# Latent attention: the rotation of the queries moved into the score's sum, and the copies of turned weights moved to one engine

## The chip, the cores and the metric

The kernel runs on one core of a Trainium2 chip. The metric is the device time of one execution in microseconds (us). A core has a matrix engine (TensorE, PE in the profile), a vector engine (VectorE, DVE), an activation engine (ScalarE, ACT), a general engine (GpSimd, POOL) and an engine that here issues the loads (SyncE, SP). Each works through its own instructions in order and waits on semaphores for the others.

## The reference, cut to what matters

One inference step of a backbone with two layers on 640 tokens (512 latent ones and 128 of a prompt). Each layer makes an adaptive norm, three attentions side by side (differential, latent, windowed), a gated merge of their outputs, and a mixture of 16 experts. The change touches the latent attention alone, which has 8 heads:

```
cq = (rms_norm(m_q, q_norm) @ mla_w_qb).reshape(B, S, 8, 64 + 32)
q_nope, q_rope = cq[..., :64], cq[..., 64:]
if latent: q_rope = apply_rope(q_rope); kr = apply_rope(kr)      # pairs (x1, x2) -> (x1 c - x2 s, x1 s + x2 c)
kv = (ckv @ mla_w_kvb).reshape(B, Sk, 8, 64 + 64)                # 64 key columns, 64 value columns a head
k = concat(kv[..., :64], kr for every head)
o = softmax(q k^T * 96 ** -0.5) v
```

Latent queries see 512 latent keys and 128 of a context (640 in all); the queries of the prompt see their own 128 keys.

## The kernel before, in words

All is fp32. In the latent attention queries and keys lie turned: features in partitions, tokens along the free dimension. A head is five steps, one for each tile of 128 queries (t = 0 to 4; t = 4 is the prompt's tile with 128 keys, the others have 640). A step i has a **score** (`mla_score`, L1029, called S below: PE writes 128x640 into `mm`), a **move** (`mla_move`, L2089: VectorE brings it into SBUF and takes the maximum), an **exponential** (`mla_exp`, L1594, on ScalarE), a **turn** (`mla_turn`, L1037, called T: five PE transposes into the one PSUM tile `tp`), a **copy** (`mla_copy`, out of `tp` into `ml_pt`, on ScalarE for even i, at L1356, and on VectorE for odd i, L2097), and, for one or two tiles together, the **values** (`mla_value`, L1049, called V, and a transpose of the inverse sums, L1053). The code writes out the order of each engine by hand: in the loop over s, PE makes the score of step s, then the turn of step s - 2, then the values of the unit that step s - 3 completes (so V falls at t = 1, 2 and 4).

Between the scores PE also prepares the next head. `project_head` has three pieces: piece 0, the queries (`product` at L749, 96 rows out, called P0), at t = 1; piece 1, the 64 key rows (L1000, P1), at t = 2; piece 2, a multiplication of the 32 query rows by a constant that swaps each pair (L1005, P2), at t = 3. ScalarE brings P0 and P1 into SBUF (`head_in`) ahead of the exponential of t = 1 and t = 2. VectorE makes the rotation of the 32 rows in `rope_head`: ahead of the move of t = 3 the swapped rows times the sine, behind that move the rows times the cosine and the sum (all at L1814). The copy of an odd step stands behind that on VectorE.

Scores and pieces share two PSUM tiles `mm`, taken in turn: the n-th user waits till the user before the last has been read (`wait_mm_empty`). A turn waits till the copy before it has emptied `tp` and till its exponential is done.

Ahead of the heads stand the rotation of the shared key rows (L974 on PE, `rope` on VectorE, and a copy to the second key buffer at L2071), and the values of all heads (`mla_v`, L987). Weights come through a ring of six slots: SP loads a chunk when the GpSimd program, by `consumed`, has counted its slot free. GpSimd computes nothing in the loops; it only counts. Chunk `qb` holds the query weights (256 rows in two halves, 768 columns), `kvb` the others.

Of the kernel before, what the change touches and what calls it, by code (L numbers as in the profile page):

```python
# [22 lines left out]
P = 128  # L23
# [5 lines left out]
TT = T // P  # L29
# [31 lines left out]
def _layout(parts):  # L61
# [9 lines left out]
    ("iota", CAP_L), ("cos64", NLAT), ("sin64", NLAT), ("cos32", NLAT), ("sin32", NLAT)])  # L71
# [7 lines left out]
def shape_constants():  # L79

    t = np.zeros((P, CONST_COLS), np.float32)

    def put(name, rows, value):
        a, b = CONST[name]
        t[rows, a:b] = value

    p = np.arange(P)
    put("ident", slice(0, P), np.eye(P))
    swap = np.zeros((P, P), np.float32)
    swap[p[1::2], p[0::2]] = -1.0  # L90
# [24 lines left out]
    put("cos32", slice(MNOPE, MQ), np.cos(a32))  # L115
    put("sin32", slice(MNOPE, MQ), np.sin(a32))
    lam = np.array([[0.8 - 0.6 * math.exp(-0.3 * l) for l in range(DEPTH)]]).T
    lam = np.concatenate([lam, 1.0 - lam], axis=1).astype(np.float32)
    return t, lam
# [47 lines left out]
def _turns(parts):  # L167
# [14 lines left out]
    ("mla_heads", MLA_N + 3 * MH), ("mla_out", 16), ("sw_kv_rot", 7),  # L182
# [88 lines left out]
def mla_s(i):  # L271


    h, t = divmod(i, TT)
    return MM["mla_heads"] + 3 + h * (TT + 3) + t + (min(t, 3) if h < MH - 1 else 0)


def mla_prep(h, piece):

    return MM["mla_heads"] + (piece if h == 0 else 3 + (h - 1) * (TT + 3) + 1 + 2 * piece)  # L280
# [48 lines left out]
def build(nc, a):  # L329
    ctx = ExitStack()  # L330
    with ctx:
# [174 lines left out]
        c_normed, kr_ready, mq_roped = sem("c_normed"), sem("kr_ready"), sem("mq_roped")  # L506
# [86 lines left out]
        def _(sp):  # L593
# [5 lines left out]
            def chunk_source(l, kind, k0, c0, width):  # L599
                r0 = k0 * P  # L600
                if kind == "qb":
                    return a["mla_w_qb"][l].rearrange("(k p) c -> p k c", p=P)
                if kind == "kvb":
                    return a["mla_w_kvb"][l]
                w = {"ada": "w_ada", "in": "w_in", "gate": "w_gate", "br_da": "w_br_da",
                     "br_mla": "w_br_mla", "br_swa": "w_br_swa", "o": "w_o"}[kind]
                return a[w][l, r0:r0 + HALF * P, c0:c0 + width].rearrange("(k p) c -> p k c", p=P)

            def chunk_target(kind, slot, width):
                if kind == "qb":  # L610
                    return ring[slot][:, :, :].rearrange("p k c -> p (k c)")[:, 0:2 * MH * MQ].rearrange(
                        "p (k c) -> p k c", k=2)
                if kind == "kvb":
                    return ring[slot][:, :, :].rearrange("p k c -> p (k c)")[:, 0:MH * (MNOPE + MV)]
                return ring[slot][:, :, 0:width]

            for l in range(DEPTH):
# [15 lines left out]
                def load(i):  # L633
                    kind, k0, c0, width = CHUNKS[i]

                    sp.wait_ge(chunks_free, l * LAYER_CHUNKS + (i + 1))
                    if i == FIRST["in"] + 2:

                        sp.dma_start(a["x_spill"], x[:, :, :]).then_inc(x_spilled, 16)
                    sp.dma_start(chunk_target(kind, i % RING, width),  # L640
                                 chunk_source(l, kind, k0, c0, width)).then_inc(slot_in[i % RING], 16)
# [50 lines left out]
        def _(pool):  # L692
# [6 lines left out]
            for l in range(DEPTH):  # L699
# [14 lines left out]
                consumed(SW_Q[3], 2)  # L714
                consumed(mla_prep(MH - 1, 2), 2)
# [17 lines left out]
        def _(pe):  # L733
# [103 lines left out]
            for l in range(DEPTH):  # L837
# [126 lines left out]
                for m in range(4):  # L964
# [15 lines left out]
                wqb = ring[FIRST["qb"] % RING][:, :, :].rearrange("p k c -> p (k c)")[:, 0:2 * MH * MQ].rearrange(  # L980
                    "p (k c) -> p k c", k=2)
# [8 lines left out]
                def project_head(hd, piece):  # L990
                    j = mla_prep(hd, piece)
                    if piece == 2:
                        wait_mm_read(pe, l, mla_prep(hd, 0))
                    wait_mm_empty(pe, l, j)
                    if piece == 0:
                        product(mm[j % 2][0:MQ, :], lambda k: wqb[:, k, hd * MQ:(hd + 1) * MQ],
                                lambda k: cq[:, k, :], 2).then_inc(mm_full[j % 2], 1)
                    elif piece == 1:
# [4 lines left out]
                    else:  # L1003
                        pe.sem_inc(pe_waited, 1)
                        pe.matmul(mm[j % 2][MNOPE:MQ, 0:NLAT], c_("swap32", slice(MNOPE, MQ)),  # L1005
                                  ml_q[hd % 2][MNOPE:MQ, 0:NLAT], start=True, stop=True).then_inc(mm_full[j % 2], 1)
# [7 lines left out]
                for piece in range(3):  # L1014
                    project_head(0, piece)
# [3 lines left out]
                def mla_score(i):  # L1019
                    hd, t = divmod(i, TT)  # L1020
                    if 1 <= t <= 3 and hd < MH - 1:
                        project_head(hd + 1, t - 1)
                    if t == 0:
                        wait_mm_read(pe, l, mla_prep(hd, 1))
                        pe.wait_ge(mq_roped, l * MH + (hd + 1))
                    j = mla_s(i)
                    wait_mm_empty(pe, l, j)
                    for lo, hi, at in latent_keys(t):
                        last = pe.matmul(mm[j % 2][:, at:at + hi - lo], ml_q[hd % 2][0:MQ, t * P:(t + 1) * P],  # L1029
                                         ml_k[hd % 2][0:MQ, lo:hi], start=True, stop=True)  # L1030
# [323 lines left out]
        def _(act):  # L1354
# [60 lines left out]
            for l in range(DEPTH):  # L1415
# [164 lines left out]
                def head_in(hd, piece):  # L1580
                    j = mla_prep(hd, piece)
                    wait_mm_full(act, l, j)
                    if piece == 0:
                        copy(ml_q[hd % 2][0:MQ, :], mm[j % 2][0:MQ, 0:T], -(MQ ** -0.5)).then_inc(mm_empty[j % 2], 1)
                    else:
                        copy(ml_k[hd % 2][0:MNOPE, :], mm[j % 2][0:MNOPE, 0:KEYS]).then_inc(mm_empty[j % 2], 1)

                head_in(0, 0)
                head_in(0, 1)
# [14 lines left out]
                for s in range(MLA_N + 2):  # L1604
                    if s < MLA_N:
                        hd, t = divmod(s, TT)
                        if 1 <= t <= 2 and hd < MH - 1:
                            head_in(hd + 1, t - 1)
                        mla_exp(s)
                    if s >= 2 and s % 2 == 0:  # L1610
                        mla_copy(s - 2)
# [200 lines left out]
        def _(dve):  # L1812
# [92 lines left out]
            for l in range(DEPTH):  # L1905
# [165 lines left out]
                dve.tensor_copy(ml_k[1][r32, :], ml_k[0][r32, :]).then_inc(kr_ready, 1)  # L2071

                def rope_head(hd, part):

                    j = mla_prep(hd, 2)
                    t_, q_ = tmp[j % 2][r32, 0:NLAT], ml_q[hd % 2][r32, 0:NLAT]
                    if part == 0:
                        wait_mm_full(dve, l, j)
                        tt(t_, mm[j % 2][r32, 0:NLAT], c_("sin32", r32), ALU.mult).then_inc(mm_empty[j % 2], 1)
                    else:  # L2080
                        tt(q_, q_, c_("cos32", r32), ALU.mult)
                        dve.drain()
                        tt(q_, q_, t_, ALU.add).then_inc(mq_roped, 1)
# [8 lines left out]

                def mla_copy(i):
                    width = T if i % TT < LT else P
                    u, n = mla_unit(i)
                    wait_t_full(dve, l, TR["mla"] + i)
                    dve.tensor_copy(ml_pt[u % 2][n][:, 0:width], tp[:, 0:width]).then_inc(t_empty, 1)  # L2097
# [28 lines left out]
                rope_head(0, 0)  # L2126
                rope_head(0, 1)
# [357 lines left out]
```

## Time and profile before

| what | before |
|---|---|
| median of 3 runs | 3476.33 us (3473.27 to 3481.16) |
| profiled execution, its own time | 3475.3 us |
| its span | 3473.5 us |
| PE busy | 3142.9 us (90%) |
| VectorE busy | 2289.6 us (66%) |
| ScalarE busy | 1699.7 us (49%) |
| GpSimd busy | 0.2 us (4 instructions) |
| mean granted PE clock | 0.953 |

The span is the time from the first instruction to the last in the trace; the execution's own time is 1.8 us longer. Busy shares are of the span. A granted clock of 1.00 is 2.4 GHz and one of 0.50 is 1.2 GHz. PE's ends are modelled, so the spacing from one PE start to the next says more than the durations do.

### The profile page before, as it was taken

What the parts mean: (1) busy time and instruction counts of PE and PEld (TensorE: products, weight loads), DVE (VectorE), ACT (ScalarE), POOL (GpSimd) and SP (SyncE); (2) the same over time, 40 slices, a digit from 0 to 9 for tenths busy, and PEclk for the clock granted to TensorE, in tenths of its full rate; (3) what the DMA queues carried; (4) which work ended last, traced back from release to release, by engine and by line L of the source; (5) the groups of instructions that cost most, each with busy time, mean ns of one, the idle gap of its engine ahead of it and who ended that gap; (6) DMA issues with size and microseconds to landing.
All of it is one profiled execution on the core that took longest, in us unless ns stands there. A gap on an engine that the chain in (4) does not pass through costs nothing.

```text
span 3473.5 us, 44790 instructions
## 1 busy us (share of the span) xinstructions
PE 3142.9 (90%) x15742; PEld 2212.6 (64%) x15742; DVE 2289.6 (66%) x3210; ACT 1699.7 (49%) x2471; POOL 0.2 (0%) x4
## 2 busy tenths in 40 slices
PE   6988998999978999999889889889899699999994
PEld 2466765667646777777636567557676477777773
DVE  6446535566548888888772654456653688888884
ACT  4425133224126777777573523331420477777773
POOL 0000000000000000000000000000000000000000
PEclk9999999999989999999899999999999799999996
DMA  8410110020217888888781001000112298888881
GB/s 298 178 55 1 60 50 1 26 87 1 103 49 257 303 296 315 314 306 314 243 316 63 31 33 52 26 25 26 63 37 91 89 322 308 308 315 313 314 313 45
DMA packets 276469, 551.00 MB, mean 159 GB/s; under 512 B 13608, under 2 KB 19424, under 8 KB 275680
## 3 DMA queue, kind: packets, MB, share of 16 engines
q1 hardware_dynamic: 273024, 543.32, 43.9%
q10 hardware_dynamic: 3296, 5.67, 0.5%
q8 instruction: 96, 1.57, 0.2%
q14 instruction: 53, 0.43, 0.0%
HBM read 537.52 MB, written 11.44 MB: 158 GB/s over the span
## 4 chain that ended last, share of the span: by engine, by line
PE 77%; DVE 9%; ACT 7%; issue 3%; DVEq 2%; ACTq 2%; DMA 0%; SPq 0%
PE mm L1281 26%; PE mm L791 14%; PE mm L749 11%; PE mm L793 4%; PE mm L853 3%; DVE w_lo L1814 2%; PE mm L821 2%; PE mm L1247 2%; PE mm L1029 2%; PE oo L1260 2%; PE oo L1049 1%; ACT scratch L1356 1%; ACTq L1750 1%; DVE tmp L1814 1%; PE mm L919 1%
## 5 line engine op out<-in xcount | busy, mean ns | idle before, releaser
L1814 DVE TENSOR_TENSOR w_lo<-ring,w_hi 128x1024 fp32r<-128x1024 f32 x864 | 1029.2, 1222 | 102.4 <-ACT w_hi L1356 82.6
L1356 ACT ACTIVATE w_hi<-ring 128x1024 fp32r<-128x1024 f32 x864 | 909.5, 1060 | 302.2 <-PE mm L1281 258.3
L1356 ACT ACTIVATE dw_hi<-ring 128x512 fp32r<-128x512 f32 (+1 forms) x168 | 104.4, 627 | 618.3 <-PE mm L793 612.9
L1814 DVE TENSOR_TENSOR dw_lo<-ring,dw_hi 128x512 fp32r<-128x512 f32 (+1 forms) x168 | 114.9, 689 | 366.1 <-ACT dw_hi L1356 365.6
L791 PE MATMUL mm<-h_hi,dw_lo 128*128 128x512 f32 (+1 forms) x672 | 327.0, 487 | 15.7 <-DVE dw_lo L1814 9.6
L793 PEld LDWEIGHTS mm<-h,ring 128*128 128x128 f32 (+1 forms) x1344 | 256.2, 191 | 61.2
L791 PE MATMUL mm<-h_hi,dw_hi 128*128 128x512 f32 (+1 forms) x672 | 269.5, 401 | 0.0
L791 PE MATMUL mm<-h_lo,dw_hi 128*128 128x512 f32 (+1 forms) x672 | 267.7, 398 | 0.0
L749 PE MATMUL mm<-scratch,ring 128*128 128x512 f32 (+3 forms) x896 | 260.2, 443 | 1.6 <-ACT scratch L1356 1.6
L793 PE MATMUL mm<-h,ring 128*128 128x128 f32 (+1 forms) x1344 | 260.5, 276 | 0.0
L749 PEld LDWEIGHTS mm<-scratch,ring 128*128 128x128 f32 (+1 forms) x896 | 141.3, 191 | 115.3 <-issue 112.9
L1281 PE MATMUL mm<-w_lo,xa_hi 128*80 128x512 f32 x512 | 202.4, 395 | 13.3 <-DVE w_lo L1814 9.3
L1281 PE MATMUL mm<-w_lo,hid_hi 128*128 128x512 f32 (+1 forms) x512 | 204.2, 399 | 3.0 <-DVE hid_lo L1814 3.0
L1281 PE MATMUL mm<-w_lo,xb_hi 128*128 128x512 f32 x512 | 202.5, 396 | 0.0
L1281 PE MATMUL mm<-w_hi,hid_hi 128*128 128x512 f32 (+1 forms) x512 | 202.5, 396 | 0.0
L1281 PE MATMUL mm<-w_hi,hid_lo 128*128 128x512 f32 (+1 forms) x512 | 202.4, 395 | 0.0
L1882 DVE RECIPROCAL tmp<-tmp 128x640 f32<-128x640 f32 x48 | 199.4, 4153 | 3.6
L1281 PE MATMUL mm<-w_hi,xa_lo 128*80 128x512 f32 x512 | 201.2, 393 | 0.0
L1281 PE MATMUL mm<-w_hi,xa_hi 128*80 128x512 f32 x512 | 199.9, 390 | 0.0
L1281 PE MATMUL mm<-w_hi,xb_hi 128*128 128x512 f32 x512 | 199.8, 390 | 0.0
L1281 PE MATMUL mm<-w_hi,xb_lo 128*128 128x512 f32 x512 | 199.1, 389 | 0.0
L1356 ACT ACTIVATE scratch<-mm 16x1024 f32<-16x1024 f32 (+8 forms) x164 | 113.0, 698 | 156.4 <-PE mm L793 44.8
(259 smaller groups left out, 5067.7 us busy)
## 6 DMA issues: line engine op xcount, KB each, us to landing
ring<-in_w_ff SPq DMA_DIRECT2D x384, 1024.0 KB, 6.0
ring<-in_w_ada SPq DMA_DIRECT2D x48, 1024.0 KB, 5.5
ring<-in_w_gate SPq DMA_DIRECT2D x24, 1024.0 KB, 6.6
ring<-in_w_in SPq DMA_DIRECT2D x16, 1024.0 KB, 10.0
ring<-in_w_o SPq DMA_DIRECT2D x8, 1024.0 KB, 7.5
x_spill<-x SPq DMA_DIRECT2D x2, 2560.0 KB, 10.6
ring<-in_w_br_da SPq DMA_DIRECT2D x4, 1024.0 KB, 6.8
ring<-in_w_br_mla SPq DMA_DIRECT2D x4, 1024.0 KB, 6.2
```

Source lines behind the costliest of these rows:

```text
L749: last = pe.matmul(out[:, lo:hi], lhs(n), rhs(n)[:, lo:hi], start=(n == 0), stop=(n == terms - 1))
L791: pe.matmul(out[0:width, 0:NLAT], w_[u % 2][:, kk, 0:width], h_[:, k, 0:NLAT], start=(k == 0 and i == 0), stop=(k == KT - 1 and i == 2))
L793: last = pe.matmul(out[0:width, NLAT:T], weight(chunk, k, c0, c0 + width), h[:, k, NLAT:T], start=(k == 0), stop=(k == KT - 1))
L821: last = pe.matmul(mm[j % 2][:, 0:width], h[:, k, t * P:(t + 1) * P], weight(chunk, k, c0, c0 + width), start=(k == 0), stop=(k == KT - 1))
L853: last = pe.matmul(mm[j % 2][0:2, 0:512], a_[:, k, :], b_[m % SPLITS][:, kk, :], start=(k == 0 and i == 0), stop=(k == KT - 1 and i == 2))
L1029: last = pe.matmul(mm[j % 2][:, at:at + hi - lo], ml_q[hd % 2][0:MQ, t * P:(t + 1) * P], ml_k[hd % 2][0:MQ, lo:hi], start=True, stop=True)
L1247: last = pe.matmul(mm[turn % 2][:, k * P:(k + 1) * P], tok[:, t, (4 * g + k) * P:(4 * g + k + 1) * P], hot[:, t, :, :].rearrange("p a s -> ...
L1260: last = pe.matmul(oo[j % 2][:, :], y[:, k * P:(k + 1) * P], hot_t[:, :], start=(i == 0), stop=(i == 1))
L1281: last = pe.matmul(out[0:rows_, bank:bank + 512], a_[:, k, 0:rows_], b_[n % SPLITS][:, kk, :], start=(k == 0 and i == 0), stop=(k == KT - ...
L1356: return act.activation(out, in_, ACT.Copy, scale=scale)
L1814: return dve.tensor_tensor(out, in0, in1, op)
L1882: dve.reciprocal(t_[:, :], t_[:, :])
```

## The change

The query weights get 128 columns a head in the ring in place of 96: columns 64 to 95 are the rotary ones, and 96 to 127 the same with each pair swapped and the first of it negated. GpSimd writes these columns, two instructions a layer, and PE waits for them (`wq_ready`). P0 then gives 128 rows: 64 plain, 32 rotary, 32 swapped. `queries_in` on VectorE multiplies the 64 rows by the scale and the other 64 by a table `turn32` (cosine, sine, and the scale in both), as it brings them into SBUF. The key buffers hold the 32 rotated key rows twice, so that the score's sum over 128 rows adds cosine part and sine part. P2, `rope_head` and the semaphore `mq_roped` fall away, and `head_in` is left with the keys alone (`keys_in`). All copies out of `tp` are ScalarE's now, and each stands ahead of the exponential of its step. The load of `qb` is split in two, in pieces of 96 columns, and the table of constants grows by 640 columns. Below, the parts stand in the order of the program: constants, SP, GpSimd (behind `consumed(SW_Q[3], 2)`), PE (the wait ahead of `mla_v`, then the pieces), ScalarE, VectorE. The new GpSimd instructions take 256 elements in each of 128 partitions, every second one.

```diff
+    ("iota", CAP_L), ("cos64", NLAT), ("sin64", NLAT), ("cos32", NLAT), ("sin32", NLAT), ("turn32", T)])
...
+    turn = np.zeros((2 * MROPE, T))
+    turn[:MROPE, :NLAT], turn[MROPE:, :NLAT], turn[:MROPE, NLAT:] = np.cos(a32), np.sin(a32), 1.0
+    put("turn32", slice(MNOPE, P), -(MQ ** -0.5) * turn)
...
-    ("mla_heads", MLA_N + 3 * MH), ("mla_out", 16), ("sw_kv_rot", 7),
+    ("mla_heads", MLA_N + 2 * MH), ("mla_out", 16), ("sw_kv_rot", 7),
...
+                    if kind == "qb":
+                        half = ring[i % RING][:, :, :].rearrange("p k c -> p (k c)").rearrange(
+                            "p (k h c) -> p k h c", k=2, h=MH)[:, 0, :, 0:MQ]
+                        sp.dma_start(half, a["mla_w_qb"][l, 0:P].rearrange("p (h c) -> p h c", c=MQ))\
+                            .then_inc(qb_in, 16)
...
+                pool.wait_ge(slot_in[FIRST["qb"] % RING], 16 * chunk_use(l, FIRST["qb"]))
+                pool.wait_ge(qb_in, l * 16 + 16)
+                pool.tensor_scalar(swapped[:, :, :, 0], rot[:, :, :, 1], -1.0, None, ALU.mult)
+                pool.tensor_copy(swapped[:, :, :, 1], rot[:, :, :, 0]).then_inc(wq_ready, 1)
                 consumed(mla_prep(MH - 1, 2), 2)
...
+                pe.wait_ge(wq_ready, l + 1)
...
-                for piece in range(3):
+                for piece in range(2):
                     project_head(0, piece)
...
-                    if 1 <= t <= 3 and hd < MH - 1:
+                    if 1 <= t <= 2 and hd < MH - 1:
                         project_head(hd + 1, t - 1)
                     if t == 0:
+                        wait_mm_read(pe, l, mla_prep(hd, 0))
                         wait_mm_read(pe, l, mla_prep(hd, 1))
-                        pe.wait_ge(mq_roped, l * MH + (hd + 1))
...
                 for s in range(MLA_N + 2):
+                    if s >= 2:
+                        mla_copy(s - 2)
                     if s < MLA_N:
                         hd, t = divmod(s, TT)
-                        if 1 <= t <= 2 and hd < MH - 1:
-                            head_in(hd + 1, t - 1)
+                        if t == 2 and hd < MH - 1:
+                            keys_in(hd + 1)
                         mla_exp(s)
-                    if s >= 2 and s % 2 == 0:
-                        mla_copy(s - 2)
...
-                dve.tensor_copy(ml_k[1][r32, :], ml_k[0][r32, :]).then_inc(kr_ready, 1)
+                dve.tensor_copy(ml_k[0][MQ:P, :], ml_k[0][r32, :])
+                dve.tensor_copy(ml_k[1][r32, :], ml_k[0][r32, :])
+                dve.tensor_copy(ml_k[1][MQ:P, :], ml_k[0][r32, :]).then_inc(kr_ready, 1)
+                def queries_in(hd):
+                    j = mla_prep(hd, 0)
+                    q_ = ml_q[hd % 2]
+                    wait_mm_full(dve, l, j)
+                    ts(q_[0:MNOPE, :], mm[j % 2][0:MNOPE, 0:T], -(MQ ** -0.5), ALU.mult)
+                    tt(q_[MNOPE:P, :], mm[j % 2][MNOPE:P, 0:T], c_("turn32", slice(MNOPE, P)), ALU.mult)\
+                        .then_inc(mm_empty[j % 2], 1)
...
-                        turned = t == 3 and hd < MH - 1
-                        if turned:
-                            rope_head(hd + 1, 0)
+                        if t == 1 and hd < MH - 1:
+                            queries_in(hd + 1)
                         mla_move(s)
-                        if turned:
-                            rope_head(hd + 1, 1)
-                    if 2 <= s < MLA_N + 2 and s % 2 == 1:
-                        mla_copy(s - 2)
```

## Rows read from the trace of the kernel before

**Rows 1.** The page, part 4: shares of the chain that ended last.

```profile
PE 77%; DVE 9%; ACT 7%; issue 3%; DVEq 2%; ACTq 2%; DMA 0%; SPq 0%
```

**Rows 2.** Windows: heads 0 to 6 of each layer (busy us, count, clock).

```profile
498.00:627.00 129.00, 112.95 (x656) 67.60 (x657) 68.59 (x195) 50.48 (x101) 0.00 (x0) 0.95 0.05 17
2198.00:2327.00 129.00, 113.02 (x657) 67.86 (x657) 68.59 (x195) 50.48 (x101) 0.00 (x0) 0.95 0.05 17
```

**Rows 3.** Timeline of PE, one head: start, us, line, count, [idle before and releaser].

```profile
552.62 1.25 PE L1029 MATMUL mm<-scratch 96*128 96x512 f32 x4
...
554.25 2.32 PE L749 MATMUL mm<-scratch,ring 128*96 128x512 f32 x8
556.41 1.25 PE L1029 MATMUL mm<-scratch 96*128 96x512 f32 x4
...
560.63 1.35 PE L1029 MATMUL mm<-scratch 96*128 96x512 f32 x4
561.81 0.71 PE L1037 MATMUL tp<-const,scratch 128*128 128x128 f32 x5
...
563.08 1.04 PE L1005 MATMUL mm<-scratch,const 32*32 32x512 f32 x2
564.05 1.35 PE L1029 MATMUL mm<-scratch 96*128 96x512 f32 x4
...
568.22 0.77 PE L1037 MATMUL tp<-const,scratch 128*128 128x128 f32 x5 [2.05 <-ACT rstd L1356]
...
570.32 1.25 PE L1029 MATMUL mm<-scratch 96*128 96x512 f32 x4
```

**Rows 4.** Timeline of VectorE, then of ScalarE, at t = 3 of that head.

```profile
565.57 0.82 DVE L2089 CUSTOM_DVE_ANT_0 scratch<-mm,scratch 128x640 f32<-128x640 f32 x1
...
567.19 0.68 DVE L1814 TENSOR_TENSOR scratch<-scratch,tmp 32x512 f32<-32x512 f32 x1
...
567.46 0.70 ACT L1356 ACTIVATE rstd<-tp 128x640 f32<-128x640 f32 x1
```

**Rows 5.** Timeline of PE: the wait of the head before it.

```profile
550.52 0.77 PE L1037 MATMUL tp<-const,scratch 128*128 128x128 f32 x5 [2.48 <-DVE pt L2097]
```

**Rows 6.** Timelines of PE and ScalarE, the start of head 0.

```profile
493.26 1.50 PE L1000 MATMUL mm<-scratch,ring 128*64 128x512 f32 x4
494.70 1.04 PE L1005 MATMUL mm<-scratch,const 32*32 32x512 f32 x2
498.07 2.39 PE L1029 MATMUL mm<-scratch 96*128 96x512 f32 x4 [2.33 <-DVE scratch L1814]
...
494.80 0.81 ACT L1356 ACTIVATE scratch<-mm 64x768 f32<-64x768 f32 x1 [0.73 <-PE mm L1000]
```

**Rows 7.** Timeline of PE: head 7's first score and the stage's last transpose.

```profile
627.04 1.66 PE L1029 MATMUL mm<-scratch 96*128 96x512 f32 x4
...
645.41 0.33 PE L1053 MATMUL oo<-const,scratch 128*128 128x128 f32 x1
```

**Rows 8.** Windows: two us behind a wait of PE.

```profile
532.00:534.00 2.00, 2.00 (x18) 1.32 (x13) 0.70 (x3) 0.00 (x0) 0.00 (x0) 0.57 0.03 8
```

**Rows 9.** Timelines of PE and VectorE, ahead of the heads.

```profile
484.08 1.04 PE L974 MATMUL mm<-scratch,const 32*32 32x512 f32 x2
485.05 5.67 PE L987 MATMUL mm<-ring,scratch 128*128 128x512 f32 x12
...
487.35 0.55 DVE L2071 COPY scratch<-scratch 32x768 f32<-32x768 f32 x1
...
490.56 0.27 PE L1011 MATMUL tp<-const,scratch 128*128 128x128 f32 x1
```

**Rows 10.** DMA issues of the first 30 us, and PE's first instruction.

```profile
const<-in_const SPq DMA_DIRECT2D x1, 1520.0 KB, 6.3
...
13.71 1.94 PE L740 MATMUL tp<-const,merged 128*128 128x128 f32 x8 [13.71 <-DMA merged<-in_x_prompt]
```

**Rows 11.** Timeline of SP: the issue of chunk qb.

```profile
418.08 0.51 SPq L640 DMA_DIRECT2D ring<-in_mla_w_qb  x1
```

More of the change, by code:

```diff
@@ L70 @@
     ("ident", P), ("swap", P), ("swap32", MROPE), ("ones", P), ("mask", 4 * P),
-    ("iota", CAP_L), ("cos64", NLAT), ("sin64", NLAT), ("cos32", NLAT), ("sin32", NLAT)])
+    ("iota", CAP_L), ("cos64", NLAT), ("sin64", NLAT), ("cos32", NLAT), ("sin32", NLAT), ("turn32", T)])
 ROWS, NROWS = _layout([
@@ L274, in mla_s @@
     h, t = divmod(i, TT)
-    return MM["mla_heads"] + 3 + h * (TT + 3) + t + (min(t, 3) if h < MH - 1 else 0)
+    return MM["mla_heads"] + 2 + h * (TT + 2) + t + (min(t, 2) if h < MH - 1 else 0)
 def mla_prep(h, piece):
-    return MM["mla_heads"] + (piece if h == 0 else 3 + (h - 1) * (TT + 3) + 1 + 2 * piece)
+    return MM["mla_heads"] + (piece if h == 0 else 2 + (h - 1) * (TT + 2) + 1 + 2 * piece)
 def mla_unit(i):
@@ L505, in build @@
         e_ready, merged_ready = sem("e_ready"), sem("merged_ready")
-        c_normed, kr_ready, mq_roped = sem("c_normed"), sem("kr_ready"), sem("mq_roped")
+        c_normed, kr_ready, wq_ready, qb_in = sem("c_normed"), sem("kr_ready"), sem("wq_ready"), sem("qb_in")
         sw_kready, sw_roped = sem("sw_kready"), sem("sw_roped")
@@ L601, in chunk_source @@
                 if kind == "qb":
-                    return a["mla_w_qb"][l].rearrange("(k p) c -> p k c", p=P)
+                    return a["mla_w_qb"][l, P:].rearrange("p (h c) -> p h c", c=MQ)
                 if kind == "kvb":
@@ L610, in chunk_target @@
                 if kind == "qb":
-                    return ring[slot][:, :, :].rearrange("p k c -> p (k c)")[:, 0:2 * MH * MQ].rearrange(
-                        "p (k c) -> p k c", k=2)
+                    return ring[slot][:, :, :].rearrange("p k c -> p (k c)").rearrange(
+                        "p (k h c) -> p k h c", k=2, h=MH)[:, 1, :, 0:MQ]
                 if kind == "kvb":
@@ L714, in _ @@
                 consumed(SW_Q[3], 2)
+                pool.wait_ge(slot_in[FIRST["qb"] % RING], 16 * chunk_use(l, FIRST["qb"]))
+                pool.wait_ge(qb_in, l * 16 + 16)
+                w_ = ring[FIRST["qb"] % RING][:, :, :].rearrange("p k c -> p (k c)").rearrange("p (n c) -> p n c", c=P)
+                rot = w_[:, :, MNOPE:MQ].rearrange("p n (i two) -> p n i two", two=2)
+                swapped = w_[:, :, MQ:P].rearrange("p n (i two) -> p n i two", two=2)
+                pool.tensor_scalar(swapped[:, :, :, 0], rot[:, :, :, 1], -1.0, None, ALU.mult)
+                pool.tensor_copy(swapped[:, :, :, 1], rot[:, :, :, 0]).then_inc(wq_ready, 1)
                 consumed(mla_prep(MH - 1, 2), 2)
@@ L979, in _ @@
                 wait_chunks(l, FIRST["qb"], 2)
-                wqb = ring[FIRST["qb"] % RING][:, :, :].rearrange("p k c -> p (k c)")[:, 0:2 * MH * MQ].rearrange(
-                    "p (k c) -> p k c", k=2)
+                wqb = ring[FIRST["qb"] % RING][:, :, :].rearrange("p k c -> p (k c)").rearrange(
+                    "p (k h c) -> p k h c", k=2, h=MH)
+                pe.wait_ge(wq_ready, l + 1)
                 wkvb = ring[FIRST["kvb"] % RING][:, :, :].rearrange("p k c -> p (k c)")[:, 0:MH * (MNOPE + MV)].rearrange(
@@ L991, in project_head @@
                     j = mla_prep(hd, piece)
-                    if piece == 2:
-                        wait_mm_read(pe, l, mla_prep(hd, 0))
                     wait_mm_empty(pe, l, j)
                     if piece == 0:
-                        product(mm[j % 2][0:MQ, :], lambda k: wqb[:, k, hd * MQ:(hd + 1) * MQ],
-                                lambda k: cq[:, k, :], 2).then_inc(mm_full[j % 2], 1)
-                    elif piece == 1:
+                        product(mm[j % 2], lambda k: wqb[:, k, hd, :], lambda k: cq[:, k, :], 2)\
+                            .then_inc(mm_full[j % 2], 1)
+                    else:
                         for lo, hi in ((0, 512), (512, KEYS)):
@@ L1002, in project_head @@
                         last.then_inc(mm_full[j % 2], 1)
[L1003 to L1006, printed above, removed]
                 pe.wait_ge(kr_ready, l + 1)
@@ L1028, in mla_score @@
                     for lo, hi, at in latent_keys(t):
-                        last = pe.matmul(mm[j % 2][:, at:at + hi - lo], ml_q[hd % 2][0:MQ, t * P:(t + 1) * P],
-                                         ml_k[hd % 2][0:MQ, lo:hi], start=True, stop=True)
+                        last = pe.matmul(mm[j % 2][:, at:at + hi - lo], ml_q[hd % 2][:, t * P:(t + 1) * P],
+                                         ml_k[hd % 2][:, lo:hi], start=True, stop=True)
                     last.then_inc(mm_full[j % 2], 1)
@@ L1578, in _, with keys_in @@
                 act.dma_start(a["new_mla_krope"][0, l], new_out[:, P:P + MROPE]).then_inc(new_sent, 16)
-                def head_in(hd, piece):
-                    j = mla_prep(hd, piece)
+                def keys_in(hd):
+                    j = mla_prep(hd, 1)
                     wait_mm_full(act, l, j)
[L1583 to L1589, printed above, removed]
+                    copy(ml_k[hd % 2][0:MNOPE, :], mm[j % 2][0:MNOPE, 0:KEYS]).then_inc(mm_empty[j % 2], 1)
+                keys_in(0)
                 def mla_exp(i):
@@ L2070, in _ @@
                 dve.drain()
-                dve.tensor_copy(ml_k[1][r32, :], ml_k[0][r32, :]).then_inc(kr_ready, 1)
[L2073 to L2083, printed above, removed]
+                dve.tensor_copy(ml_k[0][MQ:P, :], ml_k[0][r32, :])
[8 more added lines that the diff above has]
+                        .then_inc(mm_empty[j % 2], 1)
                 def mla_move(i):
@@ L2091, in mla_move @@
                                              ml_nm[:, i:i + 1]).then_inc(mm_empty[j % 2], 1)
[L2093 to L2097, printed above, removed]
                 def mla_inverse(u):
@@ L2125, in _ @@
                     dve.memset(ml_rb[b], 0.0)
-                rope_head(0, 0)
-                rope_head(0, 1)
+                queries_in(0)
                 for s in range(MLA_N + 4):
```

## The prediction, as it stood before the run

> **What bounds the kernel now.** I read the page's chain first: three quarters of it is PE, so what PE waits for, or needn't do, is what can be won [rows 1]. Then the windows over heads 0 to 6 of the latent attention: in 129 us PE works 113, VectorE 69, ScalarE 50, alike in both layers, and the clock granted is 0.95 [rows 2]. So no engine is full and PE loses 16 us of 129 to waits, and a few more to the clock. The timeline of PE shows the waits. In one head all runs on till the score of t = 4; then T2 (the turn of step t = 2) stands at 568.22 with 2.05 us of idle time ahead, released by ScalarE's copy of T1 [rows 3]. The head before waits 2.48 us at the same place, there for VectorE's copy [rows 5]. Both come from the rotation: at t = 3 VectorE moves the score (0.82) and then has the cosine product and the sum, ended at 567.87, while ScalarE has its exponential ahead of its copy, which runs from 567.46 to 568.16 [rows 4]. At the start of a layer's heads PE waits another 2.33 us for the rotation of head 0 [rows 6].
>
> **What goes.** P2 holds PE 0.97 us (563.08 to 564.05) in heads 0 to 6, and the rotation behind it goes with the waits named.
>
> **What a head costs then.** I lay the new orders out by hand from the score S2 (t = 2), as zero. The stretch from S0 to S2 keeps its instructions: 8.01 us (552.62 to 560.63) [rows 3]. Its new load is on VectorE: `queries_in`, two instructions of 640 columns out of PSUM; the nearest row is the move with 0.82 us [rows 4], so some 1.6 us. They start when P0 ends, about with S1 at 556.41. P1 waits for them (it takes the buffer of P0), but starts some 1.5 us ahead of S2, about 2.8 us behind S1's start: hidden. The move of t = 1 starts 0.6 us later than it did, and S2, which needs it read, is 4.2 us behind S1: hidden too. Without V ahead of P1 it isn't; that is head 0 alone.
>
> From S2 on: T0 starts at 1.18 (560.63 to 561.81) and is full 0.71 later, at 1.9. Here comes a **new wait**. ScalarE now has the copy of T0 first, then `keys_in`, then the exponential; S3 takes the buffer of P1 and so waits for `keys_in`. Copy 0.70 [rows 4], keys 0.81 [rows 6]: S3 can start at 3.4. PE would be ready at 2.45, which is where P2 starts now (560.63 to 563.08) [rows 3]. Wait: 1.0 us. T1 follows 1.18 behind S3, at 4.6, full at 5.3; the copy, now ahead of the exponential, ends at 6.0; T2 starts at 6.1, the prompt's short score having filled a little of the time (wait 0.75). T2 to the next S0 is 2.1 us (568.22 to 570.32). So S2 to the next S0 takes 8.2 us, where now it is 9.69 (560.63 to 570.32), and a head 16.2, where this one is 17.7. The exponential that stands behind each copy ends some 2.5 us after its score; the turn that needs it is at least 3 us behind the score in all five steps. So it costs PE nothing while PE has other pieces between; with fewer pieces (head 7) it is the copies that pace.
>
> **The clock.** In the window that follows the 2.48 us waits it is granted at 0.57, that is mostly at its lower level of 1.2 GHz, and PE's work takes double there [rows 8]; behind the wait of 2.05 in [rows 3] nothing slows (T2 to S0 is 2.1 us, five transposes, values and one more). 0.05 of 129 us is 6.5 us a layer [rows 2]. With no wait longer than 1.0 us I expect this back. It is inside the sum below, since I count in the full clock's spacing against the measured start times.
>
> **Sum a layer.** Head 0 to head 7 is now 128.97 us (498.07 to 627.04) [rows 6, 7]. Then: heads 1 to 6, 6 x 16.2 = 97.2; head 0 lacks the turns and values of a head before (2.9 us less) but waits 0.6 for `queries_in` at P1 and 0.6 more at S3: 14.6. Together 111.8, saved 17.2. Start: S0 of head 0 needs `keys_in`, which ends at 495.61, and `queries_in`, which starts with P1 at 493.26 and ends at 494.9; so it starts at 495.7 and not at 498.07: saved 2.4 [rows 6]. Head 7 is 18.4 to the last transpose (627.04 to 645.41) [rows 7]; with copies and turns laid out in the same way (S2 at 4.4, S3 at 6.7, T2 at 9.4, T3 at 11.4, T4 at 13.0) the last transpose is at 15.0: saved 3.3. That is 22.9.
>
> **What it adds.** GpSimd can't start before the last product of the windowed queries is through, which is where L974 starts (484.08), and PE now waits for it at L987, which now starts at 485.05 [rows 9]. So only 1 us of it is hidden. The trace has no arithmetic of GpSimd. Bounds for its two instructions of 256 elements: 0.2 us each at VectorE's price (a copy of 768 columns is 0.55 there [rows 9]), which hides all; and some 3 us each, 5 times that whole copy, which puts 5 us on the path. I take 1.1 each, as a slower engine with a start and an end to signal: 2.3 with the semaphore, so 1.3 us of wait. The Trainium skill, GPSIMD Engine Reference, section 4.1, speaks of one-input elementwise work there as roughly at line rate, and of two-input work as about twice as slow as VectorE's; taken as an estimate, its first clause would make the pair about 0.5 us plus dispatch, which L974 would hide, and the sum 2.6 us better. No row here can show either.
>
> The two more copies of key rows (0.55 each) end near 489.1; the transposes that wait for them stand at 490.56: hidden, by 1.4 us [rows 9]. The load of `qb` in smaller pieces is issued at 418.08 and needed at 484: 66 us of cover, against a landing of 6 to 7 us now; it would have to take ten times as long [rows 11]. The table of constants is a load of 1520 KB and grows by 320 KB; it stands in the DMA queues ahead of the tokens that PE's first instruction waits for at 13.71. It landed 6.3 us after its issue, so 320 KB are 1.3 us at most, and nothing if the tokens keep the queues no fuller; I take 0.8, since part of the 6.3 us isn't transfer [rows 10].
>
> Net: 2 x (22.9 - 1.3) - 0.8 = 42.4 us. From the profiled execution's 3475.3: 3432.9. The median of the runs is 1.0 above that execution, so 3434.
>
> **The rivals.**
> - *The clock doesn't come back* (0.16): two waits a head in place of one, each near 1 us, are 1.75 together, and the row shows a fall behind 2.48 [rows 8]. Then 6 us a layer stay: 3446.
> - *ScalarE's single order paces the heads* (0.11). It has 50.48 us in seven heads, 7.2 each; without P0 (0.7) and with two more copies (1.5) that is 8 of 16.2 [rows 2], but every exponential now waits for a turn that stands behind its own score. If a turn, a value or an inverse sum is late by that in each head, about 1.5 us: 14 x 1.5 = 21 less, 3455.
> - *The new waits are shorter than laid out* (0.08): PE alone sets the pace, 1.75 us a head less: 14 x 1.7 = 24 more, 3411.
> - *GpSimd is slow* (0.06), the case on the other side. It is one place, L987: all that PE does for the heads stands behind `wq_ready`. Beyond 1 us each us counts whole, twice. From 22 us a layer on (11 us for an instruction, twenty times VectorE's longer copy [rows 9]) the kernel is slower than before; at 10 us each it would be about 3468. An idle PE for that long would also fall to its lower clock and slow the start of `mla_v`. I give slower 0.04 of the 0.06.
> - *The change's gain doesn't reach the end*: a shorter stage could run into loads. The chain has no DMA share [rows 1] and the loads have nearly nothing to do in the heads (share 0.05 [rows 2]); this has most of the 0.05 for no change, out of the laid-out case.
>
> The laid-out case has 0.59. Its own range is 3426 to 3444 (GpSimd between its bounds, each wait by 0.3 us a head). The whole range, 3413 to 3457, takes in the first three rivals. A measurement of this kernel can't tell 0.2% (7 us) from no change: faster by more than that 0.91, within it 0.05, slower 0.04.
>
> **What would show it.** After the change: P0 to S0 in a head as before; one wait of about 1.0 us at S3, released by ScalarE, and one of about 0.75 at T2, also by ScalarE, none by VectorE; a head 16.2 us; a granted clock of 0.99 or more in the windows of heads 0 to 6; L987 2 to 3 us behind L974's start, where it is 1 now; PE's first instruction at 14.5. The prediction is wrong if L987 starts over 5 us later than now, if a head waits at T0, T3 or V, or if windows with 0.5 to 0.6 of the clock are as many as before.

## The result, and the profile after the change

| | before | changed |
|---|---|---|
| median of 4 runs | 3478.74 us | 3433.09 us (3430.31 to 3436.23) |
| profiled execution, its own time | 3475.3 us | 3435.66 us |
| its span | 3473.5 us | 3433.9 us |
| GpSimd busy | 0.2 us | 2.6 us |

The ratio is 0.9871, with a 95% interval of 0.9853 to 0.9889: 1.3% faster, 38 to 51 us. A median of 3434 was forecast, with 3413 to 3457 around it. That is a gain of 42.4 us in the forecast and one of 45.6 between the medians; the kernel before stands at 3478.74 here and not at 3476.33, since a fourth run came to its three.

First the windows over heads 0 to 6, which answer to [rows 2]: they are 112 us long in place of 129, PE works 101 of them, and the clock is 1.00.

```profile
498.00:610.00 112.00, 100.63 (x643) 63.72 (x644) 55.37 (x172) 51.66 (x110) 0.00 (x0) 1.00 0.02 7
2174.00:2286.00 112.00, 100.69 (x643) 63.76 (x644) 55.27 (x172) 51.66 (x110) 0.00 (x0) 1.00 0.02 8
```

The timeline of PE over one head, which answers to [rows 3] (L1039 is the score, L764 P0, L1014 P1, L1047 the turn, L1063 the transpose of inverse sums; the values are left out):

```profile
545.25 1.25 PE L1039 MATMUL mm<-scratch 128*128 128x512 f32 x4
...
549.04 1.25 PE L1039 MATMUL mm<-scratch 128*128 128x512 f32 x4
...
551.83 1.50 PE L1014 MATMUL mm<-scratch,ring 128*64 128x512 f32 x4
553.26 1.35 PE L1039 MATMUL mm<-scratch 128*128 128x512 f32 x4
554.44 0.71 PE L1047 MATMUL tp<-const,scratch 128*128 128x128 f32 x5
...
556.63 1.35 PE L1039 MATMUL mm<-scratch 128*128 128x512 f32 x4 [0.86 <-ACT scratch L1366]
557.82 0.71 PE L1047 MATMUL tp<-const,scratch 128*128 128x128 f32 x5
558.36 0.39 PE L1039 MATMUL mm<-scratch 128*128 128x128 f32 x2
559.32 0.77 PE L1047 MATMUL tp<-const,scratch 128*128 128x128 f32 x5 [0.57 <-ACT rstd L1366]
...
561.42 1.25 PE L1039 MATMUL mm<-scratch 128*128 128x512 f32 x4
```

From S0 to S0 are 16.17 us (545.25 to 561.42), and two waits stand in it, both released by ScalarE. The timeline of ScalarE tells why:

```profile
555.19 0.70 ACT L1366 ACTIVATE tmp<-tp 128x640 f32<-128x640 f32 x1 [2.47 <-PE tp L1047]
555.79 0.79 ACT L1366 ACTIVATE scratch<-mm 64x768 f32<-64x768 f32 x1
556.48 0.82 ACT L1600 ACTIVATE scratch<-scratch 128x640 f32<-128x640 f32 x1
...
558.56 0.70 ACT L1366 ACTIVATE rstd<-tp 128x640 f32<-128x640 f32 x1 [1.17 <-PE tp L1047]
```

The keys' copy (64x768) had its input ready since P1 ended at about 553.3, but ScalarE sat idle for 2.47 us, till T0 had filled `tp` for the copy ahead of it. S3 starts at 556.63, when the keys are in. T2 starts at 559.32, right behind the copy of T1.

Ahead of the heads, the timelines of GpSimd and of PE (L989 is L974 of before, L1003 is L987; they answer to [rows 9] and [rows 6]):

```profile
485.85 0.86 POOL L728 TENSOR_SCALAR ring<-ring 128x256 f32<-128x256 f32 x1 [485.41 <-PE mm L808]
486.65 0.41 POOL L729 COPY ring<-ring 128x256 f32<-128x256 f32 x1
...
485.45 1.04 PE L989 MATMUL mm<-scratch,const 32*32 32x512 f32 x2
487.31 5.58 PE L1003 MATMUL mm<-ring,scratch 128*128 128x512 f32 x12 [0.82 <-POOL ring L729]
...
498.06 1.32 PE L1039 MATMUL mm<-scratch 128*128 128x512 f32 x4 [1.10 <-ACT scratch L1366]
```

GpSimd's pair ends 1.6 us after L989's start, and L1003 starts 1.86 us after it, where the two stood 0.97 apart. From the values to S0 of head 0 are 10.75 us, before 13.02 [rows 6, 9].

And the end of the stage, on PE, for [rows 7]:

```profile
609.96 1.25 PE L1039 MATMUL mm<-scratch 128*128 128x512 f32 x4
...
624.84 0.33 PE L1063 MATMUL oo<-const,scratch 128*128 128x128 f32 x1
```

**Where the time came from**, in the first layer, forecast beside measured: heads 0 to 6, 17.2 us and 17.07 (128.97 less 111.90); head 7 to the last transpose, 3.3 and 3.49 (18.37 less 14.88); start, 2.4 and 2.27; GpSimd, minus 1.3 and minus 0.89. That makes 21.6 forecast, 21.94 measured. From the start of the key rotation on PE to the last transpose the stage fell by 21.9 us in the first layer and 21.6 in the second (160.96 to 139.33). The sum of 43.5 lies inside the interval for the whole; the two profiled spans differ by 39.6. The 4 us between stand outside the stage: PE reaches it 1.4 us later (484.08 before, 485.45 here), the stretch between the two stages is 1.9 us shorter, and the one from the second stage's last transpose to the end is 4.5 us longer (1128.7 and 1133.2). The change does not touch that last stretch, and over the nine profiles of this case it takes anything from 1127.3 to 1133.2 us. L989 starts at 484.02 in a second profile of the same program, so PE's arrival at the stage alone moves by 1.4 us from one execution to the next.

### The profile page after: what moved, and what is told of

Its sections match the earlier page's. It is cut to its first block, busy times and chain, and to the rows that moved or that the text cites. A ratio compares the mean times of both kernels' runs of the same rounds, so it can differ in the third digit from the quotient of the medians.

```text
span 3433.9 us, 44678 instructions
## 1 busy us (share of the span) xinstructions
PE 3117.2 (91%) x15710; PEld 2204.3 (64%) x15710; DVE 2259.4 (66%) x3158; ACT 1704.2 (50%) x2495; POOL 2.6 (0%) x8
## 2 busy tenths in 40 slices
DMA packets 280085, 551.32 MB, mean 161 GB/s; under 512 B 17736, under 2 KB 23552, under 8 KB 279296
## 4 chain that ended last, share of the span: by engine, by line
PE 78%; DVE 8%; ACT 7%; issue 3%; ACTq 2%; DVEq 2%; DMA 0%; POOL 0%; SPq 0%; POOLq 0%
PE mm L1291 26%; PE mm L806 14%; PE mm L764 11%; PE mm L808 4%; PE mm L868 4%; DVE w_lo L1820 2%; PE mm L1039 2%; PE mm L836 2%; PE mm L1257 2%; PE oo L1270 2%; ACT scratch L1366 1%; ACTq L1756 1%; PE oo L1059 1%; PE tp L1047 1%; PE mm L934 1%
## 5 line engine op out<-in xcount | busy, mean ns | idle before, releaser
L764 PE MATMUL mm<-scratch,ring 128*128 128x512 f32 (+1 forms) x896 | 258.9, 441 | 1.6 <-ACT scratch L1366 1.6
L764 PEld LDWEIGHTS mm<-scratch,ring 128*128 128x128 f32 x896 | 143.0, 194 | 112.6 <-issue 110.2
L1366 ACT ACTIVATE scratch<-mm 128x512 f32<-128x512 f32 (+8 forms) x148 | 101.5, 695 | 139.9 <-PE mm L808 44.8
```

The lines of the kernel that those rows point to most:

```text
L764: last = pe.matmul(out[:, lo:hi], lhs(n), rhs(n)[:, lo:hi], start=(n == 0), stop=(n == terms - 1))
L1366: return act.activation(out, in_, ACT.Copy, scale=scale)
```

## The experiments

All are timed against the kernel before, in runs on the same chip: its median was 3476.28 beside four of them and 3476.59 beside the other two and the changed kernel itself, which ran again with them. First that repetition:

> The changed kernel once more, beside the next two on one chip: 3430 to 3436.

Measured: 3433.7 us (3426.67 to 3436.2), ratio 0.9872 (0.9856 to 0.9889), as in the result.

**Each part alone.** First the rotation in the sum, with the copies back where they were (the first loop is ScalarE's, the line of `mla_move` VectorE's):

```diff
                 for s in range(MLA_N + 2):
-                    if s >= 2:
-                        mla_copy(s - 2)
                     if s < MLA_N:
                         hd, t = divmod(s, TT)
                         if t == 2 and hd < MH - 1:
                             keys_in(hd + 1)
                         mla_exp(s)
+                    if s >= 2 and s % 2 == 0:
+                        mla_copy(s - 2)
...
                         mla_move(s)
+                    if 2 <= s < MLA_N + 2 and s % 2 == 1:
+                        mla_copy(s - 2)
```

> The changed kernel, but the copies out of tp go back to where they were: even steps on ScalarE behind the exponential, odd steps on VectorE behind the move. Theory A (the laid-out orders decide; the copies ahead of the exponential bring nothing inside heads 0 to 6, because they open the wait at S3 that they close at T2): S3 no longer waits (keys_in is not behind a copy), T2 waits about 1.0 us in heads with VectorE's copy and 2.0 in those with ScalarE's; a head 16.0 us on the mean, head 0 to head 7 within 2 us of the changed kernel's 112; only head 7 is longer, by 2 to 3 us a layer. The time is then 3433 to 3441. Theory B (the copies are a good part of the gain): a head is over 17 us, and the time 3445 or more.

Measured: 3441.77 us (3439.98 to 3448.35), ratio 0.9901 (0.9885 to 0.9918). That is a little outside theory A and short of theory B's time. A head with VectorE's copy took 15.83 us (562.34 to 578.17 on PE's timeline), less than the changed kernel's 16.17, and S3 did not wait. But a head with ScalarE's copy took 18.48 (578.17 to 596.65), since T2 waits 2.5 us there and not 2.0. The timelines of VectorE, ScalarE and PE at that place:

```profile
589.78 0.59 DVE L1820 TENSOR_TENSOR scratch<-oo,scratch 64x128 f32<-64x128 f32 x2
590.40 0.82 DVE L2094 CUSTOM_DVE_ANT_0 scratch<-mm,scratch 128x640 f32<-128x640 f32 x1
...
591.27 0.83 ACT L1600 ACTIVATE scratch<-scratch 128x640 f32<-128x640 f32 x1 [1.91 <-DVE scratch L2094]
592.01 0.19 ACT L1600 ACTIVATION_READ_ACCUMULATOR scratch<-scratch 128x1 f32 x1
592.29 0.70 ACT L1366 ACTIVATE rstd<-tp 128x640 f32<-128x640 f32 x1
...
593.05 1.33 PE L1047 MATMUL tp<-const,scratch 128*128 128x128 f32 x5 [2.50 <-ACT rstd L1366]
```

With P2 gone S3 comes 2.35 us behind S2 and not 3.42 [rows 3], while VectorE still brings out the outputs of the unit before (589.78); so the move starts late, and the exponential and the copy behind it with it. The turn at 593.05 takes 1.33 us in place of 0.77, at the lower clock: the window from 592 to 596 has 0.61, and the heads 0.97 on the mean. So the 18.48 us hold slow clock too. In head 1 the wait is the same and no window is slow, and that head takes 16.98 us (510.92 to 527.90):

```profile
525.80 0.77 PE L1047 MATMUL tp<-const,scratch 128*128 128x128 f32 x5 [2.50 <-ACT rstd L1366]
```

So the copies ahead of the exponential do bring something within the heads, but little by the order alone: the pair with the slow window has a mean of (15.83 + 18.48) / 2 = 17.16 and the pair without it one of 16.4, against 16.17 in the changed kernel. The rest is the clock. Heads 0 to 6 take 116.1 and 115.9 us in the two layers, against 111.9, and head 7 takes 17.6 and 19.2, against 14.9; theory A had allowed 2 us for the first and 2 to 3 for the second.

The other part alone, the kernel before with every copy on ScalarE ahead of its exponential (ScalarE's loop, and the two lines that go from VectorE's):

```diff
                 for s in range(MLA_N + 2):
+                    if s >= 2:
+                        mla_copy(s - 2)
                     if s < MLA_N:
...
                         mla_exp(s)
-                    if s >= 2 and s % 2 == 0:
-                        mla_copy(s - 2)
...
-                    if 2 <= s < MLA_N + 2 and s % 2 == 1:
-                        mla_copy(s - 2)
```

> The kernel before, with all copies out of tp on ScalarE ahead of the exponential, and the rotation as it was. Theory A: T2's wait falls to 0.75 us, as in the changed kernel, and a wait of 0.9 opens at P2 (which takes the buffer of P1, read behind the copy of T0); a head 17.1 us; the 2.3 us wait at head 0 stays; head 7 is 3 us shorter; the clock in heads 1 to 6 is 1.00. Time about 3450 (3446 to 3456), so the two parts together bring less than their sum. Theory B (each part brings its own share, adding up to 42): rotation alone plus this one make 42; if the first is near 40, this one is near 3474.

Measured: 3457.88 us (3455.46 to 3460.92), ratio 0.9942 (0.9926 to 0.9959), 2 us above theory A's range and far from B. PE's timeline (L1029 score, L1005 P2):

```profile
576.38 1.35 PE L1029 MATMUL mm<-scratch 96*128 96x512 f32 x4
...
579.81 1.01 PE L1005 MATMUL mm<-scratch,const 32*32 32x512 f32 x2 [0.91 <-issue]
580.75 1.35 PE L1029 MATMUL mm<-scratch 96*128 96x512 f32 x4
...
583.44 0.77 PE L1037 MATMUL tp<-const,scratch 128*128 128x128 f32 x5 [0.57 <-ACT pt L1356]
```

The wait at T2 has fallen to what the changed kernel has, and one of 0.91 has opened ahead of P2, which takes the buffer of P1. A head is 17.17 us (585.54 to 602.71), as laid out. The view gives no releaser for this wait; that it is ScalarE's copy of P1 is argued from the order, and from what the next run does to the like wait at S3.

What the expectation missed is the clock. Besides the slow start of head 0, which the kernel before has too, it fell three times within heads 0 to 6, once in the first layer and twice in the second (the granted clock is the third number from the end, 0.52 and 0.57):

```profile
562.00:569.00 7.00, 6.63 (x37) 5.02 (x36) 3.27 (x10) 2.59 (x6) 0.00 (x0) 0.52 0.00 0
2196.00:2208.00 12.00, 10.85 (x43) 6.88 (x44) 3.57 (x9) 4.09 (x9) 0.00 (x0) 0.57 0.00 0
2289.00:2297.00 8.00, 7.63 (x44) 5.78 (x43) 3.47 (x11) 2.60 (x6) 0.00 (x0) 0.57 0.00 0
```

From P2 to P2 these heads take 19.94, 21.58 and 19.94 us in place of 17.17, some 10 us in all. Without them the time would be near 3448, inside theory A's range; so the order was laid out rightly and the clock was not. The falls came although no wait of the head was longer than the 0.91 at P2 (1.53 in the one at 2196, which is head 0). Gains of 34.5 and 18.4 us make 52.9, and together the parts bring some 43: they overlap. Both shorten the wait at T2; what else is counted twice, the clock above all, these two runs don't separate.

**The new wait, taken away.** The keys ahead of the copy:

```diff
+                    hd, t = divmod(s, TT)
+                    if t == 2 and hd < MH - 1:
+                        keys_in(hd + 1)
                     if s >= 2:
                         mla_copy(s - 2)
                     if s < MLA_N:
-                        hd, t = divmod(s, TT)
-                        if t == 2 and hd < MH - 1:
-                            keys_in(hd + 1)
                         mla_exp(s)
```

> The changed kernel with keys_in ahead of the copy of its step on ScalarE. Theory A (S3 waits only because keys_in stands behind the copy of T0): the wait of 0.86 at S3 is gone, the copy is not later since P1 is through 1.2 us before T0; a head 15.3 us, 14 x 0.86 = 12 us faster than the changed kernel, 3421. Rival (PE is held by something else just behind, so the wait moves to T1 or T2): a head stays at 16.2 or loses less than 0.4 us, time over 3427.

Measured: 3417.34 us (3412.91 to 3418.6), ratio 0.9825 (0.9808 to 0.9841), 16 us under the changed kernel by the two ratios. The rival is out, and theory A's 12 us were too few. On PE's timeline no wait is left at S3:

```profile
578.21 1.35 PE L1039 MATMUL mm<-scratch 128*128 128x512 f32 x4
...
580.56 1.25 PE L1039 MATMUL mm<-scratch 128*128 128x512 f32 x4
581.64 0.71 PE L1047 MATMUL tp<-const,scratch 128*128 128x128 f32 x5
...
583.15 0.76 PE L1047 MATMUL tp<-const,scratch 128*128 128x128 f32 x5 [0.57 <-ACT rstd L1366]
```

S2 to S3 is 2.35 us in place of 3.37 (553.26 to 556.63), and a head 15.05 (570.20 to 585.25). Six heads of 1.12 and head 0 with 1.74 (its wait at S3 was 1.48) make 8.5 us a layer, 17 in both, and that is what the rows show: heads 0 to 6 take 103.4 us in each layer, where they took 111.9. A head's 1.12 is more than the 0.86 that the wait reads: S3 is 1.02 nearer to S2, since PE's ends are modelled, and T1 starts 1.08 behind S3 (580.56 to 581.64) where it started 1.19 behind it (556.63 to 557.82).

**The clock.** An idle load on ScalarE, which changes no output, makes T2 wait a little longer than it did before the change (2.05 to 2.48):

```diff
                     if s >= 2:
+                        if s < MLA_N and s % TT == 3:
+                            for _ in range(4):
+                                copy(tmp[1][:, :], const[:, 0:T])
+                                act.drain()
                         mla_copy(s - 2)
```

> The changed kernel with four idle copies of 640 columns (constants into tmp) on ScalarE ahead of the copy at t = 3, so that T2 waits some 3 us in place of 0.75 in all 8 heads of a layer. If the clock's loss before came from the length of that one wait: windows behind it with 0.5 to 0.6 are back in several of the seven heads, mean clock over the heads 0.95 or less, and the time grows by more than the added waits (16 x 2.3 = 37 us), to 3475 to 3500. If the clock has nothing to do with it: 1.00 in the heads and 3470 or less.

Measured: one run, 3489.56 us. The wait at T2 is 2.73 us in each of the seven heads of the first layer, and the lower clock is back. PE's timeline in the first head:

```profile
512.22 1.18 PE L1047 MATMUL tp<-const,scratch 128*128 128x128 f32 x5 [2.73 <-ACT pt L1366]
```

And the windows, first the one that holds this turn, then all seven heads (the granted clock is the number behind the busy times, 0.57 and 0.94):

```profile
512.00:516.00 4.00, 3.78 (x27) 3.12 (x28) 0.39 (x2) 2.06 (x6) 0.00 (x0) 0.57 0.02 4
...
498.00:632.00 134.00, 107.58 (x640) 68.50 (x639) 55.37 (x172) 72.16 (x138) 0.00 (x0) 0.94 0.03 11
```

Of seven heads five show it (windows from 512, 532, 552, 588 and 608), two don't, behind the same wait; in the second layer six show it. A head would be 18.33 us from the added wait alone (16.17 and 2.73 less 0.57). From one T2 to the next are 18.34 us where no window between them is slow (572.03 to 590.37) and 19.9 where one is (512.22 to 532.12), so a fall of the clock costs 1.6 us. Heads 0 to 6 are 47 us longer in the two layers together: 14 x 2.16 = 30 are the added waits, and the 17 left are what eleven falls cost. Head 7 adds 10 more, and the time grew by 56. So a long wait at T2 alone is enough to bring the lower clock back. That it takes a long wait is not shown: the copies alone had it, two times out of three with no wait over 0.91 us.

**GpSimd's wait moved.** PE waits for the new columns ahead of P0 of head 0 and no longer ahead of the values (`mla_v`, which stands between the two places):

```diff
-                pe.wait_ge(wq_ready, l + 1)
...
+                pe.wait_ge(wq_ready, l + 1)
                 for piece in range(2):
                     project_head(0, piece)
```

> The changed kernel with PE's wait for GpSimd's columns moved from ahead of the values of all heads (mla_v) to ahead of P0 of head 0. GpSimd ends about 1.6 us after the start of the shared key rotation on PE, mla_v runs 5.6 us. Theory A (that wait is all that GpSimd costs): mla_v starts 1.0 us behind L989 as before the change, 0.8 us earlier than in the changed kernel, in both layers, and nothing waits for GpSimd later; 1.6 us in all, too little for the time to show. Rival (the saved time comes back at head 0, where S0 waits for keys_in or queries_in whatever comes before): S0 stays where it was, 12.6 us behind L989's start.

Measured: one run, 3427.73 us, within what single runs of the changed kernel reach (3426.67 to 3436.23). PE's timeline:

```profile
484.34 1.04 PE L989 MATMUL mm<-scratch,const 32*32 32x512 f32 x2
485.31 5.68 PE L1002 MATMUL mm<-ring,scratch 128*128 128x512 f32 x12
...
496.16 1.32 PE L1039 MATMUL mm<-scratch 128*128 128x512 f32 x4 [1.10 <-ACT scratch L1366]
```

The values start 0.97 us behind L989 again and S0 11.82 behind it, where the changed kernel has 12.61 (485.45 to 498.06): 0.79 us gone for good, so the rival is out.

**A version that beats both.** To this, P1 of the next head goes from ahead of S2 to ahead of S4, with its copy at t = 4 (first PE's order, then ScalarE's; the functions that number the users of `mm` change with it and are left out here):

```diff
-                    if 1 <= t <= 2 and hd < MH - 1:
-                        project_head(hd + 1, t - 1)
+                    if t in (1, 4) and hd < MH - 1:
+                        project_head(hd + 1, t // 4)
...
+                    hd, t = divmod(s, TT)
+                    if t == 4 and hd < MH - 1:
+                        keys_in(hd + 1)
                     if s >= 2:
                         mla_copy(s - 2)
                     if s < MLA_N:
                         mla_exp(s)
```

> The changed kernel with the wait for GpSimd later (as in the run before), and with P1 (the next head's keys) moved from ahead of S2 to ahead of S4, its copy keys_in at t = 4 ahead of the copy out of tp. Theory A (each of the two waits a head is a gap between a turn or a piece and ScalarE's copy of it, and 1.4 us of P1 between T1 and T2 fills one while the other's cause is gone): no wait in heads 1 to 6, a head 14.5 to 14.7 us, 22 to 24 us off the changed kernel, time 3407 to 3412. Rival (VectorE or ScalarE then paces: queries_in, move, inverse sums on one, copy and exponential on the other): a head stays over 15 us and a new wait for one of them shows at S1, T0 or V; time over 3414.

Measured: 3398.55 us (3397.09 to 3399.76), ratio 0.9778 (0.9761 to 0.9794), 8.5 us better than theory A's best, because a head is 14.26 us and not 14.5 to 14.7. A head on PE:

```profile
553.00 1.25 PE L1039 MATMUL mm<-scratch 128*128 128x512 f32 x4
...
561.73 1.25 PE L1039 MATMUL mm<-scratch 128*128 128x512 f32 x4
562.82 0.71 PE L1047 MATMUL tp<-const,scratch 128*128 128x128 f32 x5
563.45 1.50 PE L1013 MATMUL mm<-scratch,ring 128*64 128x512 f32 x4
564.89 0.49 PE L1039 MATMUL mm<-scratch 128*128 128x128 f32 x2
565.21 0.71 PE L1047 MATMUL tp<-const,scratch 128*128 128x128 f32 x5
...
567.26 1.25 PE L1039 MATMUL mm<-scratch 128*128 128x512 f32 x4
```

No row of it has a wait, and the head is 14.26 us. PE works 102.3 of the 103 us from 498 to 601. Heads 0 to 6 take 98.1 us in each layer against the changed kernel's 111.9, which makes 27.7 us; 1.5 come from the wait for GpSimd, and head 7 is as it was. Head 0 is in that count: its wait of 1.48 at S3 is gone, the 0.67 for VectorE now stands at S2. The 6 us that are left of the 35 stand outside the stage, in stretches that these edits don't touch, and no run explains them.

## Why the prediction was right

- *What bounds it, and the waits.* Right. All of the gain that the rows can place is in the heads' stage, and there in PE's waits, P2 and the clock.
- *The head laid out by hand.* 16.2 forecast, 16.17 measured; S0 to S2 8.01 forecast and measured (545.25 to 553.26); the wait at S3 1.0 against the 0.86 that the view reads and the 1.02 by which S3 came nearer to S2 when it was taken away, released by ScalarE; the one at T2 0.75 against 0.57, with T2 6.06 us behind S2 where 6.1 was laid out. The 8.01 rest on something that the prediction took without a reason: that a score over 128 rows costs no more than one over 96, and P0 with 128 columns no more than with 96. It holds (T0 stands 1.18 us behind S2 in both kernels). The run with the keys first shows that the copy of T0 was the cause of the first, and the one with P1 moved that 1.4 us of work between T1 and T2 covers the second.
- *That one wait closed opens another.* Half of it was seen: in the changed kernel, the copies ahead of the exponential give 1 us back at S3. Written down for the first experiment, the stronger form (they bring nothing in heads 0 to 6) fell. It left out that without P2 VectorE's move comes behind its own outputs: 16.4 us a head against 16.17 where the clock holds, 17.16 where it falls.
- *The clock.* Right in size: 1.00 in the heads, against 0.95. The reason given for it is right at most in part. The prediction read the slow window from 532 on as one behind a wait of 2.48 us; the wait ahead of it is T2's of 2.05. One behind a wait of 2.48 is at 586:

```profile
530.77 0.77 PE L1037 MATMUL tp<-const,scratch 128*128 128x128 f32 x5 [2.05 <-ACT rstd L1356]
...
586.35 0.84 PE L1037 MATMUL tp<-const,scratch 128*128 128x128 f32 x5 [2.48 <-DVE pt L2097]
...
586.00:590.00 4.00, 3.65 (x27) 3.08 (x28) 1.37 (x7) 1.20 (x3) 0.00 (x0) 0.61 0.02 4
```

  Counted over both layers before the change, a slow window follows five of the six waits of 2.48 us, one of the six of 2.05, and neither of the two of 2.37. The idle load shows that a long wait at T2 is enough. The copies alone show that it isn't needed: the clock fell there twice with 0.91 us at P2 and 0.57 at T2, nearly the waits of the changed kernel (0.86 and 0.57), which has no slow window in its heads in either profile. What that run has and the changed kernel has not is P2 and the wait ahead of it. No run takes the two apart, so whether the shorter waits or P2's going, or only both together, brought the clock back stays open.
- *GpSimd.* The term was mis-sized a little: 1.1 us each were taken, 0.86 and 0.41 measured, the wait 0.89 and 0.83 us in the two layers and not 1.3. The Trainium skill (GPSIMD Engine Reference, section 4.1) has one-input work there roughly at line rate; by the prediction's estimate from it the pair would take about 0.5 us plus dispatch, and the trace does not agree: it took 1.21 (485.85 to 487.06), and PE waited. Of the 1.86 us to L1003 some 0.4 are before its first instruction, and the trace has a row for a change of GpSimd's configuration there (11 ns, at 485.7), so the arithmetic alone is not the price.
- *The constants.* PE's first instruction came at 14.26 where it was 13.71: 0.55 us against 0.8 in the sum.
- *What was hidden* stayed so: L1021 waits for nothing behind the three key copies, and nothing waits for chunk `qb`.

The stage's gain agrees with the forecast by its terms (43.2 us forecast, 43.5 measured). That the median does so to 1 us (3434 and 3433.09) is in part luck: the stretch behind the second stage alone differs by up to 6 us from one profile to another, and the fourth run moved the median before by 2.4. The rival in which ScalarE's order paces the heads was right in kind: ScalarE sets both waits. It was less than the rival's price because they were already in the sum.

## What to carry to other kernels

Where engines work through orders written by hand, lay one period out on paper from the trace's start times, with each buffer's two users; here it gave the period to 0.03 us, new wait included, for the kernel in which the clock held. Put a copy that others wait for ahead of any instruction whose input comes later: one swap of `keys_in` and the copy was worth 16 us, more than a third of the whole change. And when a wait is closed, look for independent work that can go between the producer and the consumer that still wait: the piece moved from t = 2 to t = 4 left PE no wait in heads 1 to 6.

## What the runs showed of the hardware

- The same idle load in front of T2, a wait of 2.73 us each time, brought the lower clock in five heads of seven, and in six of seven in the second layer; a fall cost 1.6 us. Waits of 0.57 to 1.48 us a head brought none in the changed kernel, and the copies alone, where P2 is still there, had three: two with waits of 0.57 and 0.91, one with 1.53. The wait's length is not all that decides.
- A score of 640 fp32 columns took 1.18 us to the next piece whether the sum ran over 96 rows or 128. That is why the sine part could be added in the sum for nothing.
- GpSimd took 0.86 us for a multiplication by a constant and 0.41 for a copy of the same 128x256 elements with a stride of two.
- Loading 256 rows in pieces of 96 columns (384 bytes) raised the packets under 512 bytes from 13608 to 17736 and no engine waited for the load.
